# HGRN scores in a two-layer decoder trunk: one scaled array per block size instead of 16-query sub-blocks

## The reference, cut to what matters

```python
log_f = jnp.log(lb + (1.0 - lb) * jax.nn.sigmoid(f_raw))
hk = (1.0 - lb) * jax.nn.sigmoid(-f_raw)
b = jnp.cumsum(gi, axis=2)                        # of log_f, over time
diff = b[:, :, :, None, :] - b[:, :, None, :, :]
w = jnp.exp(jnp.where(causal, diff, -jnp.inf))
scores = jnp.einsum('bhtd,bhtsd->bhts', qi, w * ki[:, :, None, :, :])
```

## Time and profile before

| | |
|---|---|
| median of 3 runs | 1288.95 us (1288.56 to 1290.48) |
| profiled execution | 1287.09 us, its span 1285.1 us |
| PE busy | 993.1 us, 77% |
| DVE / ACT / POOL busy | 243.0 / 153.8 / 12.6 us |
| HBM read | 446.66 MB, 348 GB/s over the span |
| chain that ended last | DMA 48%, PE 42%, SP's queue 4%, DVE 3%, ACT 1% |

### The profile page before, as it was taken

One profiled execution on the slowest core, in us unless ns is written; L12 is line 12 of the kernel. 1 busy time (PEld: TensorE's weight loads), 2 busy tenths in 40 slices (PEclk: granted clock), 3 DMA queues, 4 the chain that ended last, 5 costly groups with the idle time before them and its releaser, 6 DMA issues.

```text
span 1285.1 us, 12164 instructions
## 1 busy us (share of the span) xinstructions
PE 993.1 (77%) x5148; PEld 433.0 (34%) x5148; DVE 243.0 (19%) x668; ACT 153.8 (12%) x320; POOL 12.6 (1%) x12
## 2 busy tenths in 40 slices
PE   5999998986767776766759987997776867767765
PEld 5657645421212121212227544542212312121211
DVE  3410225111101000101030564331101101000101
ACT  3523311100000000000021222110000000000000
POOL 0000001000000000000000000100000000000000
PEclk9988899987879878878789998998877878778878
DMA  7963067899999999999997413869999999999995
GB/s 248 302 248 131 14 279 296 341 429 427 428 429 426 429 426 429 427 428 428 417 392 255 149 69 148 340 280 430 427 428 427 428 427 428 427 429 426 429 421 218
DMA packets 62150, 448.53 MB, mean 349 GB/s; under 512 B 13072, under 2 KB 13328, under 8 KB 39568
## 3 DMA queue, kind: packets, MB, share of 16 engines
q1 hardware_dynamic: 62096, 447.73, 84.5%
HBM read 446.66 MB, written 1.05 MB: 348 GB/s over the span
## 4 chain that ended last, share of the span: by engine, by line
DMA 48%; PE 42%; SPq 4%; DVE 3%; ACT 1%; issue 1%; DVEq 0%; ACTq 0%
PE psum L519 17%; DMA ring<-in_w_up 14%; PE psum L741 11%; DMA ring<-in_w_down 10%; DMA wide<-in_w_gate 10%; DMA wide<-in_w_down 9%; DMA ring<-in_w_gate 5%; PE psum L783 5%; PE psum L736 2%; SPq L384 2%; SPq L328 1%; PE psum L475 1%; PE psum L836 1%; PE psum L482 1%; PE psum L838 1%
## 5 line engine op out<-in xcount | busy, mean ns | idle before, releaser
L519 PE MATMUL psum<-ring,mixed 128*32 128x512 f32 x1664 | 406.5, 714 | 123.8 <-DMA ring<-in_w_up 54.2
L519 PE MATMUL psum<-wide,mixed 128*32 128x512 f32 x1408 | 401.4, 710 | 108.8 <-DMA wide<-in_w_gate 62.4
L519 PEld LDWEIGHTS psum<-ring,mixed 128*32 128x32 f32 x1664 | 93.0, 128 | 328.1 <-issue 162.0
L519 PEld LDWEIGHTS psum<-wide,mixed 128*32 128x32 f32 x1408 | 88.6, 127 | 274.1 <-issue 123.2
L741 PE MATMUL psum<-ring,wide 128*128 128x512 f32 x320 | 145.5, 613 | 0.6 <-DMA ring<-in_w_in_ab 0.6
L741 PEld LDWEIGHTS psum<-ring,wide 128*128 128x128 f32 x320 | 62.3, 198 | 76.9 <-issue 75.8
L623 DVE TENSOR_TENSOR mixed<-psum,sig 128x512 f32<-128x512 f32 x16 | 16.9, 1056 | 277.9 <-PE psum L519 277.9
L482 PE MATMUL psum<-y_sb,spread 128*128 128x512 f32 x144 | 66.6, 605 | 1.6 <-DVE y_sb L628 1.6
L475 PE MATMUL psum<-sel,h 128*128 128x128 f32 x520 | 64.4, 283 | 3.5 <-DVE sel L596 3.5
L475 PEld LDWEIGHTS psum<-sel,h 128*128 128x128 f32 x520 | 61.0, 196 | 17.1 <-issue 13.4
L783 PE MATMUL psum<-ring,wide 128*128 128x512 f32 x128 | 58.7, 618 | 6.1 <-ACT wide L712 3.5
(11 more groups left out here) (238 smaller groups left out, 529.9 us busy)
## 6 DMA issues: line engine op xcount, KB each, us to landing
ring<-in_w_down SPq DMA_DIRECT2D x38, 2048.0 KB, 35.1
ring<-in_w_up SPq DMA_DIRECT2D x36, 2048.0 KB, 37.7
wide<-in_w_gate SPq DMA_DIRECT2D x34, 2048.0 KB, 36.6
ring<-in_w_gate SPq DMA_DIRECT2D x30, 2048.0 KB, 30.9
wide<-in_w_up SPq DMA_DIRECT2D x28, 2048.0 KB, 28.5
wide<-in_w_down SPq DMA_DIRECT2D x26, 2048.0 KB, 34.7
ring<-in_w_in_ab SPq DMA_DIRECT2D x8, 2048.0 KB, 16.6
ring<-in_w_in_cd SPq DMA_DIRECT2D x6, 2048.0 KB, 21.4
```

The lines of the kernel that those rows point to most:

```text
L519: mm = pe.matmul(psum[slots, out + n, :], inp[:, c, slots], slot(layer, unit)[:, at + 512 * n:at + 512 * (n + 1)], start=c == 0, stop=c == ...
```

## The change

The reference of a pair of times is now the border between two neighbouring blocks. For block width 16, 32, 64 and 128 (`LEVELS`) the 256 times fall into pairs of blocks. In one array per width, `x_level` (128 x 1024 for all heads), the first block of each pair holds the keys times exp(border − b), and the second the queries times exp(b − border). A matmul of the first block (weights) with the second (moving) gives the square of scores between them: 1 matmul of 128, 2 of 64, 4 of 32 and 8 of 16, 15 a head. The pairs within a 16-wide block keep the old reference at its 8th step: `near_k` and `near_q`, two matmuls of 128 x 128 a head, whose results outside the 16-wide blocks are overwritten by the other 15 or masked.

- ScalarE: the key's logarithm, the query's exponential and the 96 exponentials of `decayed_keys` go; six exponentials of 128 x 1024 come, for all heads at once, ahead of the query's sigmoid.
- DVE: the subtraction of line 1385 and the product of line 1394 go; two products of 128 x 1024 for `near_k` and `near_q`, eight subtractions and eight products of half that size come. The scan waits for two tables with a semaphore of their own (`consts_landed`); these two DMAs were and are the first of the small tables. The router's multiplies and the wait for the other 19 tables move behind the last `mask`.
- TensorE: 17 matmuls a head in the place of 24; the place of `scores_hgrn` in the order is the same. It waits for `near_ready`, and for all four arrays (`levels_ready`).
- GpSimd clears nothing.

TensorE at the first head, before: the names are the projection's weights (`ring`) and the scaled keys (`wide`, `h`), the numbers the partitions and the moving columns.

The diff, cut to its core:

```diff
@@ small tables, SP @@
+                sp.dma_start(consts[:, FIRST_CONSTS:], ...).then_inc(S["consts_landed"], 16)
+                sp.dma_start(masks0, ...).then_inc(S["consts_landed"], 16)
                 small_loads = [
-                    (consts[:, FIRST_CONSTS:], t["consts"][:, FIRST_CONSTS:KEPT_CONSTS]),
-                    (masks0, t["consts"][:, KEPT_CONSTS:LAYER1_CONSTS]),
@@ scores_hgrn, TensorE @@
-                for i in range(NSUB):
-                    q = q2T[:, hd, i * SUB:(i + 1) * SUB]
-                    mm = pe.matmul(psum[:, bank, i * SUB:(i + 1) * SUB], ke0[:, i, :], q, start=True, stop=True)
-                    if i >= NSUB // 2:
-                        mm = pe.matmul(psum[:, bank, SEQ - P + i * SUB:SEQ - P + (i + 1) * SUB], ke1[:, i - NSUB // 2, :], q,
-                                       start=True, stop=True)
+                for lo in range(0, SEQ, P):
+                    pe.matmul(psum[:, bank, at(lo):at(lo) + P], near_k[:, hd, lo:lo + P], near_q[:, hd, lo:lo + P],
+                              start=True, stop=True, skip_group_check=True)
+                pe.wait_ge(S["levels_ready"], len(LEVELS))
+                for width, x_level in reversed(list(zip(LEVELS, levels))):
+                    for lo in range(0, SEQ, 2 * width):
+                        mid = lo + width
+                        cols = at(mid) if width < P else P
+                        mm = pe.matmul(psum[lo % P:lo % P + width, bank, cols:cols + width], x_level[:, hd, lo:mid],
+                                       x_level[:, hd, mid:mid + width], start=True, stop=True, skip_group_check=True)
                 mm.then_inc(S["scores_done"], 1)
@@ ScalarE @@
             nc.scalar.activation(tmp, tmp, ACT.Ln).then_inc(S["f_log"], 1)
-            nc.scalar.activation(flat(k2T), flat(k2T), ACT.Ln).then_inc(S["f_log"], 1)
+            act.wait_ge(S["mid_in"], 1)
+            nc.scalar.activation(flat(near_k), tmp, ACT.Exp, scale=-1.0)
+            nc.scalar.activation(flat(near_q), tmp, ACT.Exp).then_inc(S["mid_exp"], 1)
+            for i, x_level in enumerate(levels):
+                act.wait_ge(S["level_in"], i + 1)
+                nc.scalar.activation(flat(x_level), flat(x_level), ACT.Exp).then_inc(S["level_exp"], 1)
             wait_projected(act, 2)
             nc.scalar.activation(flat(q2T), flat(proj(1)), ACT.Sigmoid).then_inc(S["q_sig"], 1)
-            decayed_keys(0)
-            decayed_keys(1)
             keep_turned(qT, 1)
             keep_values(val, 4, 1)
-            decayed_keys(2)
             keep_turned(kT, 2)
             keep_values(val2, 5, 2)
-            decayed_keys(3)
@@ DVE @@
+            for width, x_level in zip(LEVELS, levels):
+                keys, queries = sides(cumf, width)
+                key_part, query_part = sides(x_level, width)
+                border = keys[:, :, width - 1].unsqueeze(2).broadcast_to([P, HEADS * SEQ // (2 * width), width])
+                V.tensor_tensor(key_part, border, keys, ALU.subtract)
+                V.tensor_tensor(query_part, queries, border, ALU.subtract).then_inc(S["level_in"], 1)
```

More of the change, by code:

```diff
@@ L35 @@
 NSUB = SEQ // SUB
+LEVELS = (16, 32, 64, 128)
 N_GROUPS = 4
@@ L46 @@
 KEPT_CONSTS = FIRST_CONSTS + 2 * P + SEQ + 32 + N_EXPERTS
-N_SMALL = 21
+N_SMALL = 19
 RING = 6
@@ L182, in build @@
         st2 = part("mix", HEADS * TRI, "p (h n) -> p h n", h=HEADS)
-        ke0 = h[:, :, :, :].rearrange("p a b s -> p (a b) s")
-        ke1 = part("mix", NSUB // 2 * P, "p (i s) -> p i s", s=P)
+        by_head = lambda a: a.rearrange("p (h t) -> p h t", h=HEADS)
+        h_halves = h[:, :, :, :].rearrange("p a b s -> p a (b s)")
+        levels = [by_head(h_halves[:, 0, :]), by_head(h_halves[:, 1, :])]
+        levels += [part("mix", 1024, "p (h t) -> p h t", h=HEADS) for _ in range(2)]
+        near_q = part("last", 1024, "p (h t) -> p h t", h=HEADS)
         LAYER1_CONSTS = where["strict"][0]
@@ L206, in build @@
         y_sb = sb("y_sb", [P, D])[:, :]
+        near_k = by_head(y_sb)
         rt = sb("rt", [P, 512])[:, :]
@@ L1374, in _ @@
             dve.wait_ge(S["f_log"], 1)
[L1375 to L1379, removed]
+            dve.wait_ge(S["consts_landed"], 32)
             for hd in range(HEADS):
@@ L1382, in _, with sides @@
             and_wait(dve, r, S["cum_ready"], 1)
[L1384 to L1385 removed]
             sub = flat(cumf).rearrange("p (i s) -> p i s", s=SUB)
[L1388 to L1390 removed]
+            V.tensor_tensor(tmp.rearrange("p (i s) -> p i s", s=SUB), sub,
+                            sub[:, :, SUB // 2 - 1].unsqueeze(2).broadcast_to([P, HEADS * NSUB, SUB]),
+                            ALU.subtract).then_inc(S["mid_in"], 1)
+            def sides(a, width):
+                v = flat(a).rearrange("p (i b s) -> p i b s", b=2, s=width)
+                return v[:, :, 0, :], v[:, :, 1, :]
+            for width, x_level in zip(LEVELS, levels):
[4 more added lines that the diff above has]
+                V.tensor_tensor(query_part, queries, border, ALU.subtract).then_inc(S["level_in"], 1)
             dve.wait_ge(S["q_sig"], 1)
@@ L1393, in _ @@
             dve.wait_ge(S["mid_exp"], 1)
-            and_wait(dve, V.tensor_tensor(flat(q2T), flat(q2T), tmp, ALU.mult), S["qe_ready"], 1)
+            V.tensor_tensor(flat(near_k), flat(near_k), flat(k2T), ALU.mult)
+            V.tensor_tensor(flat(near_q), flat(near_q), flat(q2T), ALU.mult).then_inc(S["near_ready"], 1)
+            for i, (width, x_level) in enumerate(zip(LEVELS, levels)):
+                dve.wait_ge(S["level_exp"], i + 1)
+                for dst, src in zip(sides(x_level, width), (sides(k2T, width)[0], sides(q2T, width)[1])):
+                    r = V.tensor_tensor(dst, dst, src, ALU.mult)
+                r.then_inc(S["levels_ready"], 1)
             def rope_ret(g, col):
@@ L1437, in _ @@
             mask(7, st2[:, 3, :], const("causal_scale"))
+            dve.wait_ge(S["small_landed"], 16 * N_SMALL)
+            for l in range(2):
+                V.tensor_tensor(rw[:, l], rw[:, l], gcol[:, l, :].unsqueeze(2).broadcast_to([P, KC, 36]),
+                                ALU.mult).then_inc(S["router_ready"], 1)
             gated_norm(0, 6, 0)
```

35 lines of the change are left out of this document (10 added, 25 removed).

## The result

The changed kernel takes 1258.86 us (median of 4, 1256.66 to 1259.56) where the kernel before takes 1289.37 in the same comparison: ratio 0.9762, with a 95% interval of 0.9746 to 0.9777, 30.5 us less. Two later comparisons of the same pair gave 0.9769 (0.9747 to 0.9791) and 0.9766 (0.9741 to 0.9791), 29.9 and 30.0 us. The profiled execution took 1258.18 us (span 1256.4), 28.9 under that of before.

The account below looks back on a forecast made before the run. TensorE in layer 0's mixer was taken to gate the weights' stream. Scores 15.2, transposes 1.8, units 4 to 6 4.6 and retention 2.9 sum to 24.5 us: 1288.95 − 24.5 = 1264.4 us, range 1260 to 1273.

Parts of the forecast that it names:

- What bounds, and one for one: Layer 0's mixer: TensorE gates the weights' stream, so time taken from it between 74 and 174 us moves everything behind.
- Rival 3: Stream of weights: it does not start earlier, so the gain is hidden, 1289 us; chance 0.04.
- The clock: Layer 0's mixer: it stays full, saving 1.8 us in transposes, 4.6 in units 4 to 6, 2.9 in retention.
- Rival 1: HGRN heads 0 and 1: the clock still falls where transposes follow, 4.0 us lost, 1268.4 us; chance 0.14.
- the price of a narrow matmul: HGRN scores on TensorE: 14 narrower matmuls a head at 0.11 us each, 1.54 us of a 2.5 us head.
- from below: HGRN scores: the narrow matmuls' lower price, scaled with width: 0.11 us for 64, 0.055 for 32, 0.028 for 16, together 0.66.
- The changes of width: HGRN scores: three changes of the weights' width a head add 0.3 us, 0.1 each.
- Rival 4: HGRN scores: each of 12 width changes empties the array; decides from 2.0 us each, 1299 us at 3; chance 0.03.
- Rival 2: HGRN scores: a narrow matmul is as dear as a full one, 1270.7 us with the clock kept, else 1280; chance 0.13.
- What feeds the scores: ScalarE and DVE: arrays ready at 60.7 us, 14 us before TensorE asks at 74.5, so nothing is lost.
- The range: Whole kernel: 1260 to 1273 us, holding the forecast, rival 1 and the milder half of rival 2.
- the bound of the terms: Whole kernel: the terms' greatest saving, 19.9 + 9.7 = 29.6 us, gives 1259.4 us.

Follow-up runs that it names:

- the dense run: The kernel before, with each of its 24 matmuls a head moving 128 query columns instead of 16: 1274.75 us against 1287.12, ratio 0.9905.
- the alternating one: The changed kernel with 64-wide matmuls repeated to eight a head, in turn with the 16-wide; 17 width changes instead of 3: 1271.88 us, ratio 0.9896.
- the split wait alone: The kernel before, with the scan waiting for its two tables only and the router's multiplies behind the last mask: 1286.05 us against 1287.12.
- the last kernel: The changed kernel with units 2 to 5 issued ahead of 19 small tables and 64-wide matmuls split into 32-wide ones: 1257.45 us, ratio 0.9762.

## Why the prediction was right or wrong

- **What bounds, and one for one: right.** The 28.1 us that TensorE saved in the mixer are there at the first long wait for weights (28.35) and at the end of the profiled span (28.7). Rival 3, a hidden gain, is out.
- **The clock: right.** It stayed at 1.00 through all the stretches named. The parts outside the scores gave 8.5 us where 9.3 were forecast. The return to 128 weight columns stands in each place behind a head: transposes were 1.02 instead of 0.89, unit 6 13.93 instead of 13.75, and retention 6.07 instead of 5.7. The full effect of the clock, with what it cost inside the scores, was isolated by the dense run: 12.4 us between the medians, 12.0 in the mixer. Rival 1, a fall at heads 0 and 1, did not come. In the run with full-width weights a stretch of 3.70 + 0.92 us ahead of units 4 and 5 left the clock up; in the alternating one a stretch of 4.15 us did in head 0, and in heads 1 and 2 the clock fell at its end. So its nearness was real for stretches of that length; the changed kernel's 1.39 + 1.02 us are much shorter than any after which it fell. What the Trainium skill says of transposes (TensorE: Matmul & The Clock Gate, Part 4), that they do not count as work as matmuls do, is neither borne out nor refuted: no run took the transposes away.
- **The step that failed: the price of a narrow matmul.** I put 14 of them at 0.11 us and three changes of width at 0.1, 1.84 us a head in all. They measured 0.72, two changes within it included. That is 1.1 us too much a head and 4.4 us in all, which is more than the whole miss of the sum, 3.6 us; the clock's terms missed by 0.8 the other way. Without the two changes of 0.14 the 14 cost 0.44 us, not 1.54. I gave 0.66 us for them as the end "from below", by scaling with the width, but it was no end: the 64-wide ones cost the 0.11 that the width gives, the twelve narrowest some 0.017 us each, under the 0.028 and 0.055. The experts' matmul had shown an upper bound of 0.055 us an instruction, and I took half of it for no reason from the trace. The same row held the better clue: a matmul of 32 weight columns took 0.22 us there for 512 moving columns, where one of 128 in unit 7 takes 0.86. Why the twelve are so cheap is argued, not shown: they go to four places in turn, and seem to work side by side.
- **The changes of width: right in size, by a poor row.** 0.1 was forecast, 0.14 measured between short matmuls and 0.15 to 0.20 for the return to 128. Rival 4 needed 2.0 us each.
- **Rival 2, a narrow matmul as dear as a full one, is out.** The run with full-width weights shows what it would have been: 12.7 us more by the medians, 10.3 in the mixer.
- **What feeds the scores: right.** All was ready 3 us earlier than worked out and 16.6 us before it was read. Arrays ready 7.1 us later left the mixer at the same 101.21 us, and the split wait alone changed nothing that could be measured.
- **The range.** The errors of the sum alone do not explain a time below it: 1288.95 less the 28.1 us that the mixer saved is 1260.8, just inside. The last 2.0 us are those by which the medians' gain of 30 exceeds the mixer's, and their cause is open. The range ended at 1260 although the bound of the terms was 1259.4, and it left no room for them.

## What to carry to other kernels

With few moving columns a matmul cost here what its weights cost, so make the narrow operand the weights, and keep blocks of one width together: twelve products of 32 or fewer weight columns cost together about as much as one of 128. A slow clock can cost more behind the stretch that lowers it than within it (here 8.5 us against 3.5), so read the granted clock of the stretches after a suspicious one before pricing its removal. When an end of a range comes from scaling a price by size, ask what else could make the thing cheaper, such as work side by side.

## What the runs showed of the hardware

- Eight fp32 matmuls with 16 weight columns and 16 moving ones, 16 MATMUL records, start within 0.22 us, a change of width included. The four places in the output's partitions (0, 32, 64, 96) follow each other. That these run side by side is argued, not shown; no run put them all in one place. Records of neighbouring blocks that start in turn, in the last kernel's timeline, speak for it.
- A change of the weights' width costs 0.14 us between short matmuls (measured between 16 and 64 columns), the return to 128 columns behind a head 0.15 to 0.20 us. Between 32 and 16 columns no gap is seen in the records.
- A TensorE that was 100% busy lost the clock all the same: in the kernel before, 24 matmuls with 128 x 128 weights and 16 moving columns did so in every head, and the same 24 with 128 moving columns took 5.36 to 5.59 us a head at 1.00.
- One kernel's executions differ by where the clock stands: 27.9 or 29.7 to 30.0 us for the first two units (hidden where TensorE then waits for unit 2), 3.84 or 5.40 for the gather of layer 0, 27.9 or 29.9 to 30.0 at layer 1's start. A fourth place, 14.0 or 16.7 to 17.0 us at its output projection, looks like the largest swing and is none: it is paid back within what follows, down to 0.5 us. So compare the start of a later stretch too before booking such a difference.
